# A two-block transformer kernel: modulation sums, forget biases, accumulation banks and last attention units rearranged in the mixer

## What is computed

```python
mod = silu(c) @ w_ada + b_ada              # 1024 x 6144, split in sh1, sc1, g1, sh2, sc2, g2
h = rmsnorm(x) * (1 + sc1) + sh1
z = h @ w_in                               # q, k, v of mixers A, B, C, forget, indexer, gates
# A: chunked attention, table bias; 4 heads of 64
# B: causal attention + cumsum(log_sigmoid(fb + b_forget)); 4 heads
# C: the top 64 keys of an indexer; 4 query heads, one key/value head
y = (g0 * (ya @ w_branch[0]) + g1 * (yb @ w_branch[1]) + g2 * (yc @ w_branch[2])) @ w_out
x = x + g1 * rmsnorm(y)
```

## Time and profile before

| | |
|---|---|
| runs | 831.87, 834.47, 835.8 us; median 834.47 |
| the profiled execution's own time | 831.32 us |
| its span | 829.5 us |
| granted clock over the span | 0.975 |
| busy | TensorE 759.9, VectorE 539.7, ScalarE 410.4, POOL 72.0 us |
| DMA | 139.6 MB, mean 168 GB/s |

### The profile page before, as it was taken

One profiled execution on the slowest core, in us unless ns is written; L12 is line 12 of the kernel. 1 busy time (PEld: TensorE's weight loads), 2 busy tenths in 40 slices (PEclk: granted clock), 3 DMA queues, 4 the chain that ended last, 5 costly groups with the idle time before them and its releaser, 6 DMA issues.

```text
span 829.5 us, 14372 instructions
## 1 busy us (share of the span) xinstructions
PE 759.9 (92%) x6064; PEld 738.1 (89%) x6064; DVE 539.7 (65%) x776; ACT 410.4 (49%) x551; POOL 72.0 (9%) x62
## 2 busy tenths in 40 slices
PE   2499989889789899999999999999899999999995
PEld 2499989888788799999999989999889999999994
DVE  4967978777564587777756357926666465566654
ACT  4275534545244554444443437527445445555633
POOL 0110000000220100000000020000014332221000
PEclk9799999999899999999999999979999999999998
DMA  9965375577234055555565615513516553223001
GB/s 354 417 216 197 107 297 207 206 276 279 102 102 153 28 195 192 198 173 184 198 248 215 207 62 196 198 58 107 196 53 201 197 178 128 102 102 138 17 1 51
DMA packets 20952, 139.63 MB, mean 168 GB/s; under 512 B 2356, under 2 KB 2996, under 8 KB 5016
## 3 DMA queue, kind: packets, MB, share of 16 engines
q1 hardware_dynamic: 20600, 137.80, 46.1%
q0 software_dynamic: 288, 0.92, 0.3%
HBM read 137.66 MB, written 1.05 MB: 167 GB/s over the span
## 4 chain that ended last, share of the span: by engine, by line
PE 57%; DVE 7%; ACT 6%; issue 3%; POOL 1%; ACTq 0%; DVEq 0%
PE res L1378 16%; PE res L1379 16%; PE res L1380 16%; ACT whi L559 2%; PE pS L1539 2%; PE pX L1561 2%; DVE wlo L903 1%; PE pX L1726 1%; DVE y L1130 1%; POOL sq L479 1%; DVE hlo L930 1%; ACT L587 1%; PE pT L1549 1%; ACT sq L574 1%; PE pX L1465 1%
## 5 line engine op out<-in xcount | busy, mean ns | idle before, releaser
L1378 PE MATMUL res<-hhi,whi 128*128 128x256 f32 (+1 forms) x1168 | 339.0, 290 | 9.5 <-DVE hlo L930 6.6
L903 DVE TENSOR_TENSOR wlo<-raw,whi 128x2048 fp32r<-128x2048 f32 (+1 forms) x106 | 237.8, 2244 | 148.9 <-ACT whi L559 147.3
L1379 PE MATMUL res<-hhi,wlo 128*128 128x256 f32 (+1 forms) x1168 | 332.0, 284 | 0.0
L1380 PE MATMUL res<-hlo,whi 128*128 128x256 f32 (+1 forms) x1168 | 331.7, 284 | 0.0
L559 ACT ACTIVATE whi<-raw 128x2048 fp32r<-128x2048 f32 (+1 forms) x106 | 198.1, 1870 | 168.7 <-issue 128.8
L1378 PEld LDWEIGHTS res<-hhi,whi 128*128 128x128 f32 (+1 forms) x1168 | 224.3, 192 | 13.5 <-issue 6.1
L1379 PEld LDWEIGHTS res<-hhi,wlo 128*128 128x128 f32 (+1 forms) x1168 | 224.5, 192 | 0.3
L1380 PEld LDWEIGHTS res<-hlo,whi 128*128 128x128 f32 (+1 forms) x1168 | 224.2, 192 | 0.2
L1378 PE MATMUL res<-uhi,whi 128*128 128x256 f32 x176 | 49.9, 283 | 0.0
L1379 PE MATMUL res<-uhi,wlo 128*128 128x256 f32 x176 | 49.3, 280 | 0.0
L1380 PE MATMUL res<-ulo,whi 128*128 128x256 f32 x176 | 49.3, 280 | 0.0
(11 more groups left out here) (282 smaller groups left out, 1144.1 us busy)
## 6 DMA issues: line engine op xcount, KB each, us to landing
raw<-in_wts SPq DMA_DIRECT2D x100, 1024.0 KB, 5.0
raw<-in_w_ada SPq DMA_DIRECT2D x16, 1024.0 KB, 4.8
gates<-in_w_ada SPq DMA_DIRECT2D x6, 1024.0 KB, 8.4
raw<-in_wts SPq DMA_DIRECT2D x4, 768.0 KB, 7.1
y<-in_w_ada SPq DMA_DIRECT2D x2, 1024.0 KB, 10.9
x<-in_xT SPq DMA_DIRECT2D x2, 512.0 KB, 6.1
outT<-x SPq DMA_DIRECT2D x4, 256.0 KB, 2.0
biasA<-in_relb SPq DMA_DIRECT2D x1, 768.0 KB
```

The costliest lines, as they stand in the source:

```text
L903: nc.vector.tensor_tensor(wlo[c % SPL][:, 0:b], raw[RAW_OF["w", c] % RAW][:, 0:b], whi[c % SPL][:, 0:b].bitcast(f32), ALU.subtract).then_i ...
L1378: mm(out, ah, bh, start=first, stop=False)
L1379: mm(out, al, bh, start=False, stop=False)
L1380: return mm(out, ah, bl, start=False, stop=last)
```

## The change

Of the twelve slices, two are now loaded behind VA and KB, three behind WOUT + 2, WOUT + 3 and UP, the others behind seven of the ZG chunks; the sums follow two stages ahead. In the unit stages a sum stands between the even slot and the odd one. All four forget biases are made in stage KB, in the four quarters of `pS`. V is kept with 128 columns per head, 64 of them zero, so that both heads of a pair accumulate into the same columns of one bank: `pO` for mixers A and C, `pX` for mixer B. `yhi` and `ylo` are one instruction per mixer, and only unit 16 waits for a `ylo`. Units 24, 25 and 26 stand behind products 1 and 3 of BRANCH and product 1 of BRANCH + 1; VectorE's slot 27 stands ahead of the last product of BRANCH + 1. `gtmp` has four buffers. The last top-k rounds move from stage ZG + 1 to ZG + 3. (Left out below: renumbered counts of `pad_set` and `misc_ready`, and the body of VectorE's `unit_slot`, which moves unchanged but for `ylo`.)

```diff
-ADA_AFTER = {ZG + i: 8 + i for i in range(12)} | {DOWN + 3 * i: 20 + i for i in range(4)}
+ADA_AT = (VA, KB, ZG + 1, ZG + 2, ZG + 4, ZG + 5, ZG + 7, ZG + 8, ZG + 10, WOUT + 2, WOUT + 3, UP)
+ADA_AFTER = {c: 8 + i for i, c in enumerate(ADA_AT)} | {DOWN + 3 * i: 20 + i for i in range(4)}
...
-            qkv = {n: sb(f"m_{n}", [P, 2, T], at=st) for n in ("qa", "va", "qb", "vb", "qc", "qi")}
-            miscf = sb("miscf", [MW, T], at=st)
+            qkv = {n: sb(f"m_{n}", [P, 2, T], at=st) for n in ("qa", "qb", "qc", "qi")}
             kkp = sb("kkp", [P, 4, T], at=st)
-            vc2 = sb("vc2", [P, 2, P], at=st)
+            va4, vb4 = sb("va4", [P, 4, 2, P], at=st), sb("vb4", [P, 4, 2, P], at=st)
+            vc2 = sb("vc2", [P, 2, 2, P], at=st)
...
-        gtmp = sq[:, 0:4, :].rearrange("p a b -> p (a b)").rearrange("p (r n) -> p r n", r=2)
+        gtmp = sq[:, :, :].rearrange("p a b -> p (a b)").rearrange("p (r n) -> p r n", r=4)
+        miscf = logvar[0:MW, :]
...
+            for values in (vc2, va4, vb4):
+                own(nc.gpsimd.memset(values[:, :, 0, 64:128], 0.0))
+                nc.gpsimd.memset(values[:, :, 1, 0:64], 0.0).then_inc(pad_set, 1)
...
-                                                gtmp[:, n % 2, :].rearrange("p (a b) -> p a b", a=2), ALU.add
+                                                gtmp[:, n % 4, :].rearrange("p (a b) -> p a b", a=2), ALU.add
...
-                        nc.scalar.activation(vc2[:, :, :].rearrange("p t (d n) -> p t d n", d=2),
-                                             both[:, :, None, 0:64].to_broadcast([P, 2, 2, 64]), ACT.Copy).then_inc(misc_ready, 1)
+                        for e in range(2):
+                            nc.scalar.activation(vc2[:, :, e, 64 * e:64 * e + 64], both[:, :, 0:64], ACT.Copy).then_inc(misc_ready, 1)
...
+                    elif b in (VA, VB):
+                        dst = va4 if b == VA else vb4
+                        for e in range(2):
+                            v = ps[:, :].rearrange("p (r e n) -> p r e n", r=4, e=2)[:, :, e, :]
+                            nc.scalar.activation(dst[:, :, e, 64 * e:64 * e + 64], v, ACT.Copy
+                                                 ).then_inc(drained_act if e else act_self, 1)
+                        act_count[0] += 1
...
-                        nc.scalar.activation(yhi[0:64, m, :], pO[0:64, :], ACT.Copy).then_inc(act_self, 1)
-                        nc.scalar.activation(yhi[64:128, m, :], pX[64:128, :], ACT.Copy).then_inc(y_hi, 1)
-                        act_count[0] += 1
+                        nc.scalar.activation(yhi[:, m, :], pX[:, :] if m == 1 else pO, ACT.Copy).then_inc(y_hi, 1)
...
                 if c == BRANCH:
-                    for s in (24, 25, 26, 27):
-                        unit_slot(s)
+                    unit_slot(24)
+                    unit_slot(25)
+                if c == BRANCH + 1:
+                    unit_slot(27)
...
+
+                def unit_slot(s):
+                    if s % 8 == 3 and s > 8:
+                        m = s // 8 - 1
+                        dve.wait_ge(y_hi, m + 1)
+                        nc.vector.tensor_tensor(ylo[:, m, :], pX[:, :] if m == 1 else pO, yhi[:, m, :].bitcast(f32),
+                                                ALU.subtract).then_inc(y_lo, 1)
...
+                if c == BRANCH:
+                    unit_slot(24)
                 if BRANCH <= b < WOUT:
                     for j in range(4):
                         n = 4 * (b - BRANCH) + j
+                        if n == 7:
+                            unit_slot(27)
...
                         else:
-                            dst = gtmp[:, n % 2, :]
-                            if n >= 6:
-                                dve.wait_ge(merged, n - 5)
+                            dst = gtmp[:, n % 4, :]
+                            if n >= 8:
+                                dve.wait_ge(merged, n - 7)
...
-                if b in (KB, VB):
-                    for h in ((0, 1) if b == KB else (2, 3)):
-                        dve.wait_ge(bB_done, h + 1)
-                        ps = pS[:, 512 * (h % 2):512 * (h % 2) + T]
+                if b == KB:
+                    for h in range(4):
+                        dve.wait_ge(bB_done, 2 * (h // 2) + 2)
+                        ps = pS[:, T * h:T * h + T]
                         own(nc.vector.tensor_tensor(biasB[:, h, 0:P], ps[:, 0:P], cmask[:, 0:P], ALU.add))
                         nc.vector.tensor_tensor(biasB[:, h, P:384], ps, cmask[:, P:384], ALU.add).then_inc(bB_ready, 1)
-                    if b == VB:
-                        dve.wait_ge(bB_ready, 4)
-
...
-                        nc.vector.tensor_tensor(ylo[0:64, m, :], pO[0:64, :], yhi[0:64, m, :].bitcast(f32), ALU.subtract
-                                                ).then_inc(dve_self, 1)
-                        nc.vector.tensor_tensor(ylo[64:128, m, :], pX[64:128, :], yhi[64:128, m, :].bitcast(f32), ALU.subtract
-                                                ).then_inc(y_lo, 1)
-                        dve_count[0] += 1
...
+                    dve.wait_ge(bB_ready, 4)
 
                 if ZG <= c < BRANCH:
                     unit_slot(2 * (c - ZG))
-                    unit_slot(2 * (c - ZG) + 1)
                 if b + 2 in ADA_AFTER:
                     ada(ADA_AFTER[b + 2])
-                if b in (ZG, ZG + 1):
-                    for i in range(4 + 2 * (b - ZG), 6 + 2 * (b - ZG)):
+                if ZG <= c < BRANCH:
+                    unit_slot(2 * (c - ZG) + 1)
+                if b in (ZG, ZG + 3):
+                    for i in ((4, 5) if b == ZG else (6, 7)):
                         topk_round(1, i)
-                if c == BRANCH:
-                    for s in (24, 25, 26, 27):
-                        unit_slot(s)
...
-                        pe.wait_ge(bB_ready, 3 + s)
+                        pe.wait_ge(bB_ready, 2 * s + 2)
...
-                    out = pX if h % 2 else pO
+                    out = pX[:, :] if m == 1 else pO
                     pe.wait_ge(pT_ready, u + 1)
-                    if u % 8 == 0 and m:
-                        pe.wait_ge(y_lo, m)
+                    if u == 16:
+                        pe.wait_ge(y_lo, 1)
                     for i in range(t + 1):
-                        v = (qkv["va"], qkv["vb"])[m][:, i, P * (h // 2):P * (h // 2) + P] if m < 2 else vc2[:, i, :]
-                        last = mm(out[:, T * (h // 2) + t * P:T * (h // 2) + t * P + P], v,
-                                  upT[:, u % 2, P * i:P * i + P], start=i == 0, stop=i == t)
+                        v = (va4, vb4)[m][:, 2 * i + h // 2, h % 2, :] if m < 2 else vc2[:, i, h % 2, :]
+                        last = mm(out[:, T * (h // 2) + t * P:T * (h // 2) + t * P + P], v, upT[:, u % 2, P * i:P * i + P],
+                                  start=i == 0 and h % 2 == 0, stop=i == t and h % 2 == 1)
...
-                    if c in (KB, VB):
+                    if c == KB:
                         pe.wait_ge(fcum_ready, 1)
                         pe.wait_ge(idx_relu, 8)
                         pe.wait_ge(mixc_in, 80)
-                        for h in ((0, 1) if c == KB else (2, 3)):
-                            if h >= 2:
-                                pe.wait_ge(bB_ready, h - 1)
-                            mm(pS[:, 512 * (h % 2):512 * (h % 2) + T], sel[:, P * h:P * h + P], fgate[:, 4, :],
+                        for h in range(4):
+                            mm(pS[:, T * h:T * h + T], sel[:, P * h:P * h + P], fgate[:, 4, :],
                                start=True, stop=True).then_inc(bB_done, 1)
...
-                        if b == 0 and j < 3:
-                            units(24 + j)
+                        if (b, j) in ((0, 1), (0, 3), (1, 1)):
+                            units((24, 25, 26)[2 * b + j // 2])
```

More of the change, by code:

```diff
@@ L637, in _ @@
                         act_count[0] += 1
+                    elif b in (VA, VB):
[5 more added lines that the diff above has]
+                        act_count[0] += 1
                     else:
-                        dst = qkv[("qa", "", "va", "qb", "", "vb")[b - QA]]
+                        dst = qkv["qa" if b == QA else "qb"]
                         nc.scalar.activation(dst[:, :, :].rearrange("p a b -> p (a b)"), ps[:, :], ACT.Copy
@@ L721, in _ @@
                         if j == 0:
-                            act.wait_ge(pad_set, 4)
+                            act.wait_ge(pad_set, 7)
                         if j >= 2:
@@ L1017, in _ @@
                 b = c - 1
+                def unit_slot(s):
[4 more added lines that the diff above has]
+                                                ALU.subtract).then_inc(y_lo, 1)
+                    if s < 24:
+                        m, t, h = s // 8, s % 8 // 4, s % 4
+                        nk, a = P * (t + 1), P * t
```

(48 more changed lines are left out.)

2 lines of the change are left out of this document (1 added, 1 removed).

## The result

| kernel | runs | median us | range us | ratio to before, 95% interval |
|---|---|---|---|---|
| before | 4 | 835.12 | 831.87 to 835.8 | |
| changed | 4 | 822.52 | 818.62 to 823.87 | 0.9859 [0.9834, 0.9883] |

The change makes the kernel 12.6 us faster; forecast were 15.2.

What follows compares the result with a forecast made beforehand. TensorE was taken as the bound, with holes and clock falls of 24.2 us in reach. Terms +0.64 - 8.6 - 8.85 = -16.8, with clock +1.6 giving -15.2: 834.5 to 819.3 us, range 812.5 to 828.

Steps and rivals of the forecast that it cites:

- The forget biases at once: Stage KB: four biases made together, so units(0) no longer waits; -1.51 us, +0.64 net with the scan's +2.45.
- the clock term: Behind TensorE's 2.9 us pause before 94.85: a fall to half clock, taken as +1.6 us, bounds 0 and 3.4.
- Unit stages: Fewer sums, placed between slots, banks in turn: -12.8 us of holes and falls, +4.2 of new waits, -8.6 net.
- The loop through the odd slot: Unit stages with sums: ScalarE's split queues behind the odd slot, making 8.45 us against TensorE's 7.2; waits of 4.2 us.
- Branch chunks: Last units over two branch chunks, four gtmp buffers: 23.3 us instead of 32.15, so -8.85, bounds -4 and -10.
- I kept the 0.64: End of branch chunks: low split beside POOL's adds stays at 2.93 us instead of 2.29, not up to 2.6 us later.
- What was costed at nothing: Sums in QA and W_out, VB's load 0.3 us late, extra POOL memsets, V copied in two: no cost.
- Cover 4.7 us, cost nothing: W_out: three sums end about 260, before the norm at 264.98, in VectorE's idle time; without that cover 2.45 us.
- The clock stays down: Rival, 0.03: pause before 94.85 drops the clock to 1.2 GHz, short waits keep it there; held through, about 867 us.
- The loop pays in full: Rival, 0.2: each sum between slots costs 1.25 us, 8.8 not 4.2, branch end gives 4 of 8.85; 828.7 us.
- nothing is won: Rival, 0.05, in the stages: 2.45 us at the scan with a 3.4 fall, weights late each stage; about 832 us.
- Nearly all goes: Rival, 0.15: no clock fall at 95 and the loop hides; -21 us, 813.5 us.

Runs made afterwards that it cites:

- e5: e2 with the bias matmuls of heads 2 and 3 moved to the middle of VB, so two groups instead of one; 816.53 us, ratio 0.9794.
- e12: e11 with the bias matmuls in two groups as in e5; 814.03 us, ratio 0.9762.
- e2: Changed kernel with the forget scan made ahead of stage QB's low split and indexer sums; 816.74 us, ratio 0.9787.
- e3: Changed kernel with 12 dummy matmuls filling TensorE's wait for the forget scan; 820.02 us, ratio 0.9828.
- e4: Changed kernel with the modulation sum behind both unit slots of a stage instead of between them; 820.46 us, ratio 0.9838.
- e6: Changed kernel with even heads in pO and odd in pX for all mixers again, with the ylo waits before units 8 and 16; 825.3 us, ratio 0.99.
- e9: Changed kernel with the twelve sums loaded behind ZG to ZG + 11 again, eleven made in unit stages, still between the slots; 824.35 us, ratio 0.9879.
- e10: e9 with each sum behind both slots, as in e4; 822.49 us, ratio 0.9861.
- e7: Changed kernel with units 24 to 26 and slots 24 to 27 bunched early in BRANCH as before, four gtmp buffers kept; 826.97 us, ratio 0.9919.
- e11: Changed kernel with e2's and e4's edits, and POOL's add for product 7 behind the last branch chunk's low split; 812.34 us, ratio 0.9753.
- e8: Changed kernel with two gtmp buffers instead of four; 822.77 us, ratio 0.9853.

## Why the prediction was right or wrong

**The scan: right, +2.4 for +2.45.** VectorE in the changed kernel has no slack from VA to QB, as the prediction had it, and the sum of VA delays the scan by its own length; the wait is 2.78 us for the "about 2.8" forecast.

**The forget biases at once: right in the work, and the clock term failed.** The step is the line "I take +1.6, the nearest row, since the pause stands alone". Without a fall, e5 and e12 reach units(0) in 11.1 us, forecast were 10.9. The changed kernel takes 15.0: the fall is 10.2 us long, longer than the 6.8 that I had as the upper bound, and costs 3.9 us. Of that 2.7 to 2.8 go with the pause (e2, e3), 1.2 with the eight thin matmuls in a row (e5, e12). The pause's part is that of one execution: behind the same pause, e4 lost 1.5 us and e6 nothing, so some of the miss is the chance of the profiled execution. The part of the thin matmuls I hadn't foreseen at all: I counted them as the same four biases in another place. Before, they had stood in two pairs. (e9 and e10 have the bunched biases and the old scan, and show it by itself: 12.3 us with the fall of 3.4.) Whether the pause alone, or pause and thin matmuls together, made the longer falls isn't separated: no run has the pause with the biases in two groups.

**Unit stages: right, -9.4 for -8.6.** The parts stand as walked. Waits for transposes came to 3.0 us, forecast as 4.2, five of them up to 1.0, and no `ylo` wait. TensorE in the changed kernel, the three longest of them:

```profile
129.78 0.30 PE L1523 MATMUL pT<-ident,up 128*128 128x128 f32 x1 [0.89 <-ACT upT L697]
...
168.34 0.41 PE L1523 MATMUL pT<-ident,up 128*128 128x128 f32 x2 [0.96 <-ACT upT L697]
...
176.69 0.30 PE L1523 MATMUL pT<-ident,up 128*128 128x128 f32 x1 [0.66 <-ACT upT L697]
```

The two falls went with their holes, and TensorE's busy time fell from 88.4 to 85.2. The loop through the odd slot is real but small, 1.1 us by e4; it grows to 3.5 where every stage has a sum (e9 less e10), where the rival of the full loop would have had 1.25 for each, 13.8. The runs don't say by themselves what else takes up the rest.

**Branch chunks: right in kind, 1.95 us short** (-6.9 for -8.85). The spreading gave 4.2 us (e7) and the falls went (clock 1.00). The waits of 0.55 and 0.47 are those forecast as 0.6 for a bank and 0.5 for the last `ylo` (it ends at 214.60, TensorE goes on at 214.70); the 0.4 in chunk two didn't come. One step that failed is "I kept the 0.64": the low split beside POOL's adds lost 1.11 us, so a bank came 1.13 us late where I had 0.4, and W_out starts 2.85 us after the last product where I had 2.15. e11 takes the overlap away and gets 1.6 us back: no late bank, and 2.31 us at the end. The Trainium skill (SBUF — State Buffer, Who interferes with whom), which I had named and not followed, has the first of the two instructions hold the shared read port to its end while the other waits; here the split, issued 0.04 us behind the start of an add of 1.29, lost 1.11 of it, nearly one whole add, between my value and the two adds for which I had worked the rule out. But this is only half of the miss: waits and end came to 2.15 + 2.85 = 5.0 us where I had 1.9 + 2.15 = 4.05. The other 1.0 us lies in the products and units between the waits: they took 20.25 us, and the 23.3 of the forecast leave 19.25 for them. I had no term for it, and which of my steps took it off stays open. Four buffers instead of two have no part in it (e8): VectorE's split meets an add either way.

**What was costed at nothing** was nothing ahead of the units, but not behind W_out. The sum of QA lies in VectorE's gap, and the split behind it waits 0.57 us for ScalarE where it had waited 2.97. VectorE in the changed kernel, then ScalarE's split of VB:

```profile
73.10 1.28 DVE L928 CUSTOM_DVE_ANT_0 raw<-raw,cact,cols 128x1024 f32<-128x1024 f32 x1
...
76.16 2.29 DVE L915 TENSOR_TENSOR wlo<-raw,whi 128x2048 fp32r<-128x2048 f32 x1 [0.57 <-ACT whi L564]
...
88.98 1.28 DVE L928 CUSTOM_DVE_ANT_0 raw<-raw,cact,cols 128x1024 f32<-128x1024 f32 x1
...
254.79 0.17 DVE L1133 SCALAR_TENSOR_TENSOR pcol<-mod,cols 128x8 f32<-128x8 f32 x1
255.62 0.48 DVE L1141 SCALAR_TENSOR_TENSOR y<-y,pcol,rstd 128x256 f32<-128x256 f32 x1 [0.66 <-ACT rstd L592]
```

```profile
80.42 1.91 ACT L564 ACTIVATE whi<-raw 128x2048 fp32r<-128x2048 f32 x1 [2.73 <-DMA raw<-in_wts]
```

VB's split waits for its load, which now stands behind a sum; it is ready in time all the same. The sums in the W_out stages aren't hidden. The norm still waits for `rstd` and not for them, by 0.66 us, but `rstd` is itself late: the norm starts 30.81 us behind the start of W_out, 30.15 before. What I left out is the load queue. ScalarE's last split ahead of the norm waits for its weights, and the drains of the last W_out products stand behind that split. ScalarE in the changed kernel, then in the kernel before, where the last drain had 4.55 us to spare:

```profile
247.90 1.91 ACT L564 ACTIVATE whi<-raw 128x2048 fp32r<-128x2048 f32 x1 [8.19 <-DMA raw<-in_wts]
249.72 0.58 ACT L716 ACTIVATE sq<-res 128x512 f32<-128x512 f32 x1
```

```profile
252.61 1.91 ACT L559 ACTIVATE whi<-raw 128x2048 fp32r<-128x2048 f32 x1 [2.83 <-issue]
...
260.04 0.60 ACT L704 ACTIVATE sq<-res 128x512 f32<-128x512 f32 x1 [4.55 <-PE res L1380]
```

In all eleven profiles with the three sums there, that split waits 8.2 to 9.8 us for its load and the norm comes 0.6 to 2.7 us late; in the three without them (before, e9, e10) it starts at 30.15. The total pays in full: less this delay, the rest is 593.4 to 593.6, 594.6 to 594.9 or 595.9 to 596.0 us, by whether the clock is at half for 6.8, 10.2 or 13.7 us near 530. So the term "Cover 4.7 us, cost nothing" failed; it looked at VectorE's idle time alone. The extra memsets on POOL end long before its first multiply, which still has 6.07 us of idle ahead.

**Rivals.** "The clock stays down" fell: one fall behind the pause, then 1.00 through 88 us. "The loop pays in full" and "nothing is won" fell with the unit stages. "Nearly all goes" needed a loop that hides and no fall: the waits came to 3.0 us, not 0, and the fall came. That e11 ends at 812.3, near its 813.5, is a coincidence of other edits.

By term, in the two profiles: of 5.9 us missed, 2.5 are the stretch to units(0), nearly all of it clock, 1.95 the branch chunks, 1.6 the chance of the start, 0.7 the norm behind W_out, less 0.8 gained in the units. By medians 2.6 us are missed, as the profiled execution of before was one of its faster ones. So the forecast total is closer than its terms: clock and branch chunks were given too little, the load queue behind W_out nothing, and the medians hide part of that.

## What to carry to other kernels

When work is moved off a crowded engine, look at what is queued behind its *new* place: here a 2.4 us sum ahead of a 0.7 us scan that TensorE waits for cost about 5 us, somewhat less than half of it as clock, and moving the scan ahead of it gave all of that back. Price a hole on TensorE as its length plus the half speed behind it, as a range and not from one profile: the same 2.8 us wait brought 0 to 3.0 us more. Don't bunch thin matmuls just because their count stays the same. When a load moves in a shared ring of buffers, walk the loads behind it too, and what is queued behind the instruction that waits for them: three sums that fitted into VectorE's idle time still made a norm up to 2.7 us late. Where two engines read in parallel, check whether an instruction on the critical path overlaps one that could as well come later: one more wait, on POOL, made the kernel 1.6 us faster there.

## What the runs showed of the hardware that I had not expected

- The granted clock fell to half for 3.4 us in a stretch in which TensorE was busy without a hole (3.10 of 3.10 us in e2, at 1.00), at eight fp32 matmul instructions with 4 rows in a row. All eleven profiles with these eight in a row had a fall, during them or within about 1 us behind them; with the same instructions in two groups none of three had (before, e5, e12).
- The same wait of 2.76 to 2.78 us on TensorE, between the same instructions, was followed by half speed of 10.2 us (four profiles), 6.8 (e4) or only the 3.4 of the thin matmuls (e6): 15.2 to 12.3 us for the same work.
- The same edit-free first 60 us came out with half-speed periods of 13.7 us, 13.7 and 3.4, or 17.1 and 3.4, worth up to 2.4 us of span, in no relation to the kernel that I can see.
- A VectorE instruction of 128 x 2048 with two inputs, 2.29 us alone, took 3.40 us when it was issued into a running POOL add of 1.29 us.
